# Expert visits written out: token widths by rank of count, and gate/up weight pieces of two k-tiles by 1024 columns

## The reference

```
logits = (xt @ router).astype(jnp.float32)
top_vals, top_idx = lax.top_k(logits, TOP_K)
gates = jax.nn.softmax(top_vals, axis=-1)
combine = jnp.sum(jax.nn.one_hot(top_idx, N_EXPERTS) * gates[..., None], axis=1)
for e in range(N_EXPERTS):
    y_e = (silu(xt @ w_gate[e]) * (xt @ w_up[e])) @ w_down[e]
    y = y + combine[:, e:e + 1] * y_e
```

## Time and profile before

| | us |
|---|---|
| median of three runs | 1701.02 (1700.5 to 1705.84) |
| span of the profiled execution | 1701.5 |
| from its start to the first matmul of visit 0 | 708.0 |
| the eight visits | 964.2 |
| from there to the end | 29.3 |

### The profile page before, as it was taken

How to read it: one execution, slowest core, us unless ns; L and a number is a source line. 1 busy time by engine, 2 the same in 40 slices (tenths; PEclk the granted TensorE clock), 3 DMA queues, 4 the chain that set the end, 5 groups by cost and what they waited for, 6 DMA issues and landing times.

```text
span 1701.5 us, 41732 instructions
## 1 busy us (share of the span) xinstructions
PE 1564.4 (92%) x17645; PEld 1289.8 (76%) x17645; DVE 1394.4 (82%) x1389; ACT 1093.8 (64%) x985; POOL 316.3 (19%) x401
## 2 busy tenths in 40 slices
PE   6969798999887978799999999999999999999996
PEld 4858687888766867688778787787877887887884
DVE  4869977555684997799899899899898998997994
ACT  4646365444445545577777677777777777777773
POOL 2689711000178961000000000000000000000000
PEclk9979899999998989799999999999999999999998
DMA  9634455456452535299999999999999999999980
GB/s 308 231 119 149 161 178 174 142 199 230 141 213 80 175 121 202 76 367 383 344 371 392 325 376 391 334 380 392 318 385 388 332 382 348 351 393 339 360 332 26
DMA packets 204414, 463.93 MB, mean 273 GB/s; under 512 B 8062, under 2 KB 10238, under 8 KB 204204
## 3 DMA queue, kind: packets, MB, share of 16 engines
q1 hardware_dynamic: 201724, 455.38, 74.0%
q0 software_dynamic: 1760, 4.50, 1.0%
q10 hardware_dynamic: 752, 1.32, 0.2%
HBM read 459.74 MB, written 2.89 MB: 272 GB/s over the span
## 4 chain that ended last, share of the span: by engine, by line
PE 64%; DVE 15%; issue 7%; POOL 7%; ACT 5%; DMA 1%; SPq 1%; DVEq 0%; ACTq 0%; POOLq 0%
PE ps L679 20%; PE ps L681 20%; PE ps L680 20%; DVE w_lo L1420 3%; DVE w_lo L1849 3%; DVE arena L1535 3%; ACT w_hi L1371 2%; POOL stat L557 2%; DMA stage<-in_w_in 1%; PE ps L947 1%; DVE z L1840 1%; POOL arena L581 1%; POOL arena L567 1%; ACT w_hi L1094 1%; POOL stat L565 1%
## 5 line engine op out<-in xcount | busy, mean ns | idle before, releaser
L1849 DVE SCALAR_TENSOR_TENSOR w_lo<-stage,w_hi 128x2048 f16<-128x2048 f32 x330 | 750.5, 2289 | 96.5 <-ACT w_hi L1371 96.4
L1371 ACT ACTIVATE w_hi<-stage 128x2048 f16<-128x2048 f32 x330 | 629.4, 1910 | 213.3 <-PE ps L681 212.3
L679 PE MATMUL ps<-arena,w_hi 128*128 128x128 f16 (+1 forms) x3952 | 711.6, 225 | 22.5 <-issue 20.8
L681 PE MATMUL ps<-arena,w_lo 128*128 128x128 f16 (+1 forms) x3952 | 711.6, 225 | 0.7 <-issue 0.6
L680 PE MATMUL ps<-arena,w_hi 128*128 128x128 f16 (+1 forms) x3952 | 711.6, 225 | 0.0
L679 PEld LDWEIGHTS ps<-arena,w_hi 128*128 128x128 f16 x3952 | 388.9, 98 | 37.2 <-issue 26.4
L680 PEld LDWEIGHTS ps<-arena,w_hi 128*128 128x128 f16 x3952 | 389.0, 98 | 10.2
L681 PEld LDWEIGHTS ps<-arena,w_lo 128*128 128x128 f16 x3952 | 389.0, 98 | 6.6 <-issue 1.2
L679 PE MATMUL ps<-xh,w_hi 128*128 128x264 f16 x1184 | 337.5, 285 | 56.6 <-ACT arena L1238 21.3
L1420 DVE SCALAR_TENSOR_TENSOR w_lo<-stage,w_hi 128x2048 f16<-128x2048 f32 (+1 forms) x106 | 239.4, 2282 | 142.5 <-ACT w_hi L1094 142.3
L680 PE MATMUL ps<-xl,w_hi 128*128 128x264 f16 x1184 | 337.2, 285 | 0.0
(11 more groups left out here) (280 smaller groups left out, 1191.8 us busy)
## 6 DMA issues: line engine op xcount, KB each, us to landing
stage<-in_moe_w_gate SPq DMA_DIRECT2D x112, 1024.0 KB, 7.7
stage<-in_moe_w_up SPq DMA_DIRECT2D x112, 1024.0 KB, 8.0
stage<-in_moe_w_down SPq DMA_DIRECT2D x112, 1024.0 KB, 7.6
stage<-in_w_in SPq DMA_DIRECT2D x44, 1024.0 KB, 5.5
stage<-in_ffn_w_gate SPq DMA_DIRECT2D x10, 1024.0 KB, 5.4
stage<-in_ffn_w_up SPq DMA_DIRECT2D x10, 1024.0 KB, 5.3
stage<-in_ffn_w_down SPq DMA_DIRECT2D x10, 1024.0 KB, 5.3
stage<-in_w_out SPq DMA_DIRECT2D x8, 1024.0 KB, 5.5
```

The source lines that it names most:

```text
L679: mm(out, ah, bh, start=start, stop=False, skip_group_check=True)
L681: return mm(out, al, bh, start=False, stop=stop, skip_group_check=True)
L1371: fn(w_hi[:, n % SLOTS, :], stage[:, n % SLOTS, :], ACT.Copy, scale=WS).then_inc(S["hi_done"], 1)
L1849: V.scalar_tensor_tensor(w_lo[:, n % SLOTS, :], stage[:, n % SLOTS, :], WS, w_hi[:, n % SLOTS, :], ALU.mult, ALU.subtract).then_inc(S["lo_ ...
```

## The change

The loop over visits becomes a loop over **rounds**, `Fori(0, nr)`, and the eight visits of a round are written out in its body, each with constants of its own. Visit v has a **width** `CAPS[v]`: 128, 128, 104, 96, 88, 80, 72, 64. Gather, gate and up matmuls, activations and outputs take only so many token columns. Visit 0 is always expert 0; the other seven are sorted by falling count, so that visit 1 is the fullest. VectorE does the sorting before visit 0 (`sort_experts`) and writes the order to `order_i`, which SP reads before the loads of each visit from 1 on. The number of rounds is 1 when every sorted count is within its width, 2 or 3 when one is over its width or over twice its width.

The counts above give 89 for visit 0 and 120, 86, 66, 53, 44, 38, 32 for the others.

Chunks are taken in pairs, `BLOCKS`: (0, 1), (2, 3), (4, 5) and 6 alone. A gate or up piece of a pair has 2 k-tiles by 1024 columns, so 4 KB runs as the down pieces have; those of chunk 6 stay 4 k-tiles by 512 columns. A visit still has 42 pieces of 1 MB, of which 38 have runs of 4 KB (14 before), and the same number of matmuls. Activations of a pair are done one after the other, and `hh`, `hl` hold four chunks instead of two. `y_rows` shares its place with buffers of the visits.

```
+CAPS = [128, 128, 104, 96, 88, 80, 72, 64]
+ROUNDS = 3
-VISIT = 6 * NC
+BLOCKS = [[c for c in (b, b + 1) if c < NC] for b in range(0, NC, 2)]
+def n_pieces(b):
+    return 2 * len(BLOCKS[b])
 def visit_order():
     order = []
-    for c in range(NC):
-        order += [(kind, c, h) for kind in "gu" for h in range(2)]
-        if c:
-            order += [("d", c - 1, h) for h in range(2)]
-    return order + [("d", NC - 1, h) for h in range(2)]
+    for b in range(NB):
+        order += [(kind, b, q) for kind in "gu" for q in range(n_pieces(b))]
+        if b:
+            order += [("d", b - 1, q) for q in range(n_pieces(b - 1))]
+    return order + [("d", NB - 1, q) for q in range(n_pieces(NB - 1))]
...
# SP
-            with sp.Fori(0, NE) as v:
-                visit(v)
+            def visits(r):
+                for v in range(NE):
+                    if v == 0:
+                        e = slice(0, 1)
+                    else:
+                        sp.wait_ge(S["order_ready"], 1)
+                        e = bass.ds(sp.value_load(order_i[0:1, v:v + 1], min_val=1, max_val=NE - 1), 1)
+                    for m in range(VISIT):
+                        n = PRE + m
+                        sp.wait_ge(S["lo_done"], so_far((r, v), VISIT, n - SLOTS + 1))
+                        load(*visit_piece(e, m), n % SLOTS)
...
# TensorE
+                for i, c in enumerate(cs):
+                    b = c % 2 + (0 if kind == "g" else 2)
...
+                    for j in range(4):
+                        for k in range(nk):
+                            kk = nk * q + k
+                            t = mm3(ps[:, b, j * cap:(j + 1) * cap],
+                                    wh(slot, k, 512 * i + j * P, 512 * i + (j + 1) * P, 512 * len(cs)),
+                                    wl(slot, k, 512 * i + j * P, 512 * i + (j + 1) * P, 512 * len(cs)),
+                                    xgh[:, kk, 0:cap], xgl[:, kk, 0:cap], kk == 0 and j == 0, kk == KT - 1)
...
+            with pe.Fori(0, nr) as r:
+                for v in range(NE):
+                    at = (r, v)
+                    gate_up(at, 0)
+                    scatter(at, 0)
+                    gate_up(at, 1, "g")
+                    scatter(at, 1)
+                    gate_up(at, 1, "u")
...
+                    down(at, 0)
+                    for blk in range(2, NB):
+                        gate_up(at, blk)
+                        down(at, blk - 1)
+                    if v < NE - 1:
+                        gather((r, v + 1), at)
...
# VectorE, before visit 0
+                own.then(V.scalar_tensor_tensor(count[:, 1, :], count[:, 0, :], float(NE), idx_w, ALU.mult, ALU.add))
+                own.then(V.tensor_tensor(of, key.unsqueeze(1).to_broadcast(sq), key.unsqueeze(2).to_broadcast(sq),
+                                         ALU.is_gt))
+                own.then(V.tensor_reduce(count[:, 2, 1:], of, X, ALU.add))
...
+                V.tensor_copy(order_i[:, 1:], count[:, 5, 1:]).then_inc(S["order_ready"], 1)
```

More of the change, by code:

```diff
@@ L499, in _ @@
                     sp.dma_start(x_rows[:, :, 512:D], rows[:, :, 512:D]).then_inc(S["ld_x2"], 16)
[L501 to L506, removed]
-            with sp.Fori(0, NE) as v:
-                visit(v)
+            def visits(r):
[9 more added lines that the diff above has]
+                        load(*visit_piece(e, m), n % SLOTS)
+            visits(0)
             sp.wait_ge(S["visits_ready"], 1)
[L512 to L515, removed]
+            nr = sp.value_load(visits_i[0:1, 0:1], min_val=1, max_val=ROUNDS)
+            with sp.If(nr > 1):
+                with sp.Fori(1, nr) as r:
+                    visits(r)
             sp.nop()
@@ new lines, in _, with slot_of, piece @@
+            nr = pe.value_load(visits_i[0:1, 0:1], min_val=1, max_val=ROUNDS)
+            def slot_of(m):
+                return (PRE + m) % SLOTS
+            def piece(at, kind, blk, q):
+                cap = CAPS[at[1]]
+                m = order.index((kind, blk, q))
+                slot = slot_of(m)
+                cs = BLOCKS[blk]
+                nk = KT // n_pieces(blk)
+                pe.wait_ge(S["lo_done"], so_far(at, VISIT, PRE + m + 1))
+                end = q == n_pieces(blk) - 1
+                for i, c in enumerate(cs):
+                    b = c % 2 + (0 if kind == "g" else 2)
+                    if q == 0:
+                        pe.wait_ge(*in_visit(bank_free, b, at, c // 2 - 1))
+                    for j in range(4):
[5 more added lines that the diff above has]
+                                    xgh[:, kk, 0:cap], xgl[:, kk, 0:cap], kk == 0 and j == 0, kk == KT - 1)
+                    if end:
+                        t.then_inc(bank_full[b], 1)
+                if not end:
+                    t.then_inc(S["part_used"], 1)
@@ new lines, in gate_up, with down @@
+            def gate_up(at, blk, kinds="gu"):
+                if blk == 0:
+                    for b in (6, 7, 1, 3):
+                        pe.wait_ge(*in_visit(bank_free, b, at, -1))
+                for kind in kinds:
+                    for q in range(n_pieces(blk)):
+                        piece(at, kind, blk, q)
+            def down(at, blk):
+                cap = CAPS[at[1]]
+                for q in range(n_pieces(blk)):
+                    m = order.index(("d", blk, q))
+                    slot = slot_of(m)
+                    end = blk == NB - 1 and q == n_pieces(blk) - 1
+                    c = BLOCKS[blk][q // 2]
+                    pe.wait_ge(S["e_split"], so_far(at, NC, c + 2))
+                    pe.wait_ge(S["lo_done"], so_far(at, VISIT, PRE + m + 1))
+                    for half in range(2):
+                        b = 4 + half
+                        if blk == 0 and q == 0:
+                            pe.wait_ge(*in_visit(bank_free, b, at, 1))
+                        for k in range(2):
+                            f = 2 * (q % 2) + k
+                            cols = slice(f * cap, (f + 1) * cap)
+                            t = mm3(ps[0:cap, b, :], hh[:, c % 4, cols], hl[:, c % 4, cols],
+                                    wh(slot, k, half * 512, half * 512 + 512, D),
+                                    wl(slot, k, half * 512, half * 512 + 512, D),
+                                    c == 0 and f == 0, c == NC - 1 and f == 3)
+                        if end:
+                            t.then_inc(bank_full[b], 1)
+                    if not end:
+                        t.then_inc(S["part_used"], 1)
@@ L1811, in gather_lo @@
+            def gather_lo(cap, wait):
                 for h in range(2):
```

419 lines of the change are left out of this document (218 added, 201 removed).

## The result

The changed kernel takes **1630.35 us** (median of four runs, 1629.04 to 1635.01) beside 1702.9 for the kernel before on the same chip (1700.5 to 1705.84): a ratio of 0.958, with a 95% interval of 0.956 to 0.960. The forecast was 1628 in a range of 1603 to 1662. The profiled execution has a span of 1628.8 us.

What follows compares the result with a forecast made beforehand. The prediction took TensorE to bound all eight visits before, and transfers to bind visits 2 to 7 after. Start 712.9, visits 0 and 1 233.1, visits 2 to 7 652, end 29.3: 1627.3, stated as 1628 us, range 1603 to 1662.

Runs made afterwards that it cites:

- e2: The changed kernel with chunks taken one at a time, so gate and up pieces keep 2 KB runs, widths as in the change: 1659.94 us.
- e4: The changed kernel with widths that only just hold the counts (96, 120, 88, 72, 56, 48, 40, 32): 1619.18 us.
- e3: The changed kernel with only the writing out left: all widths 128, single chunks with 2 KB runs, no sort: 1669.93 us.
- e1: The changed kernel with all eight widths 128; sort, paired pieces and written-out visits stay: 1670.55 us.
- e6: The changed kernel with VectorE converting only half of the columns of each low weight piece in the visits: 1626.02 us.
- e5: The changed kernel with each load of the visits bringing only half of the k-tiles of its piece: 1598.0 us.

## What to carry to other kernels

Where three resources stand within a tenth of each other, cost a change by the next wall and not by what it saves on the first: here 14 to 36 us of TensorE's work a visit (1344 matmuls, 24 to 64 columns less, 0.419 ns each) were worth 6 to 9, because transfers stood at 110 and VectorE at 105. An edit that looks nearly idle alone (long runs, about 5) can bring six times as much beside another (29.6, from e2 to the change), so single ablations should be read as a table and not added, and all corners should have the same fixed parts. And cost the end of a loop separately, from the last landing to the last matmul, counting every piece that is still queued on each engine and what the program puts behind it.

## What the hardware showed that I had not expected

- **A floor under narrow matmuls, with full weight loads.** In e4 at a clock of 1.00 the matmuls of 32 columns start 25.0 ns apart, 40 steps in 1.00 us, where the slope of 0.419 ns a column would give 15.5:

```profile
1534.31 0.18 PE L718 MATMUL ps<-arena,w_hi 128*128 128x32 f16 x1
...
1535.31 0.18 PE L719 MATMUL ps<-arena,w_lo 128*128 128x32 f16 x1
```

  At a clock of 0.50 it is 26.7 ns, which is 32 columns at 1.2 GHz:

```profile
1514.84 0.19 PE L717 MATMUL ps<-arena,w_hi 128*128 128x32 f16 x1
...
1515.56 0.19 PE L717 MATMUL ps<-arena,w_hi 128*128 128x32 f16 x1
```

  (27 steps in 0.72 us). The Trainium skill, "TensorE: Matmul & The Clock Gate", section "Wait — 56ns, not 53.3ns?", has the same floor, about 25 ns from start to start, and the trace agrees. Its section "LDWEIGHTS (loading the stationary operand)" would give each load of 128 columns 107 ns; here each of these matmuls has its own load and still follows after 25, so that figure is not the price of a load in a row of loads.
- **The length of a run sets the rate of a full queue.** 386 GB/s in e2, where 28 of 42 pieces have 2 KB runs, 403 with 4, and 407 to 410 in stretches of 4 KB runs alone. The DMA share is 1.02 or 1.03 in all of them, and 1.02 as well in e3 at 379 GB/s, where TensorE was the bound: the share does not tell a full queue, the time to landing does.
- **The time to landing is a measure of slack, not of speed.** For an up piece it is 8.2 us before the change and 8.2 to 8.4 in e3 and e1, where TensorE is the bound; 10.7 in the changed kernel and 12.3 in e6, at the same 403 and 404 GB/s.
- **An engine can be full.** VectorE is busy for 599.55 of 600 us in e5, with six slots between it and its neighbours and the transfers at half of their bytes.
